# Eight weight halves of layer two's modulation: from the routing stage to the border of the layers

## The reference

```
silu_c, silu_cc = silu(c), silu(c_ctx)
for l in range(2):
    sh1, sc1, g1, sh2, sc2, g2 = split(silu_c @ w_mod[l] + b_mod[l], 6)     # the same for silu_cc
    u = h * (1 + sc1) + sh1                    # input of the token mixer
    h = layer_norm(alpha * h + g1 * token_mixer(u), ...)
    u2 = h * (1 + sc2) + sh2                   # input of the experts
    h = layer_norm(alpha * h + g2 * grouped_moe(u2), ...)
```

## Time and profile before

| | |
|---|---|
| median of 3 runs | 1628.79 us (1627.73 to 1631.53) |
| the profiled execution, its own time | 1631.92 us |
| its span (first to last instruction) | 1630.1 us |
| experts of layer one | 685 to 972 us |
| border: last product to layer two's first product | 972 to 996 us |
| mean granted clock of TensorE | 0.979 |

### The profile page before, as it was taken

How to read it: one execution, slowest core, us unless ns; L and a number is a source line. 1 busy time by engine, 2 the same in 40 slices (tenths; PEclk the granted TensorE clock), 3 DMA queues, 4 the chain that set the end, 5 groups by cost and what they waited for, 6 DMA issues and landing times.

```text
span 1630.1 us, 31680 instructions
## 1 busy us (share of the span) xinstructions
PE 1526.6 (94%) x13300; PEld 977.2 (60%) x13300; DVE 871.1 (53%) x1553; ACT 371.3 (23%) x893; POOL 272.4 (17%) x303
## 2 busy tenths in 40 slices
PE   6999999899999999898999886999999998999984
PEld 2454576564444468665666455767678887566642
DVE  3159946576777743652336437494552126554445
ACT  1100047541000010422222122003651002121211
POOL 0300000101112300043334330000000000543321
PEclk9999999999999999999999997999999998999998
DMA  9533220105857952999669968443125467999993
GB/s 338 176 103 94 78 68 27 49 30 180 277 151 249 319 209 80 354 414 391 235 270 400 414 273 304 143 120 99 47 59 190 144 220 284 375 415 414 414 415 137
DMA packets 147455, 365.23 MB, mean 224 GB/s; under 512 B 11265, under 2 KB 90729, under 8 KB 130419
## 3 DMA queue, kind: packets, MB, share of 16 engines
q1 hardware_dynamic: 125536, 296.86, 49.1%
q0 software_dynamic: 19328, 60.62, 11.0%
q10 hardware_dynamic: 2451, 5.73, 1.2%
HBM read 356.66 MB, written 10.62 MB: 225 GB/s over the span
## 4 chain that ended last, share of the span: by engine, by line
PE 66%; DVE 5%; DMA 5%; ACT 2%; SPq 1%; issue 1%; POOL 1%; DVEq 0%; ACTq 0%; POOLq 0%
PE psum L1166 64%; DMA yab<-in_moe_w_gu 3%; DMA arena<-in_moe_w_gu 1%; SPq L931 1%; PE psum L1703 1%; DVE ring L2772 1%; PE psum L1450 0%; DVE st L2197 0%; DMA yab<-ys 0%; DVE H L2794 0%; DVE st L2198 0%; POOL qkT_mqk L1076 0%; PE psum L1272 0%; DVE H L2210 0%; ACT uT L1870 0%
## 5 line engine op out<-in xcount | busy, mean ns | idle before, releaser
L1166 PE MATMUL psum<-uT,ring 128*128 128x512 f32 (+1 forms) x1440 | 496.1, 503 | 6.3 <-DMA ring<-in_w_in 4.8
L1166 PEld LDWEIGHTS psum<-uT,ring 128*128 128x128 f32 x1440 | 273.9, 192 | 216.4 <-issue 194.7
L1166 PE MATMUL psum<-ring,mo_tok 128*32 128x256 f32 x4992 | 312.9, 385 | 22.5 <-DVE ring L2772 22.2
L1166 PEld LDWEIGHTS psum<-ring,mo_tok 128*32 128x32 f32 x4992 | 158.8, 111 | 126.1 <-DVE ring L2772 30.1
L1166 PE MATMUL psum<-ring,v_tok 128*32 128x256 f32 x2496 | 150.1, 381 | 0.5 <-ACT v_tok L2119 0.5
L2350 DVE SCALAR_TENSOR_TENSOR convT<-upad_extra,cwT,convT 128x512 f32<-128x512 f32 (+1 forms) x240 | 132.4, 614 | 2.1
L1166 PEld LDWEIGHTS psum<-ring,v_tok 128*32 128x32 f32 x2496 | 82.3, 111 | 54.3 <-issue 1.7
L1166 PE MATMUL psum<-ring,uT 128*128 128x256 f32 (+1 forms) x576 | 113.1, 357 | 0.0
L1166 PEld LDWEIGHTS psum<-ring,uT 128*128 128x128 f32 x576 | 99.4, 191 | 15.4 <-issue 4.2
L1166 PE MATMUL psum<-yab,ring 128*128 128x512 f32 (+1 forms) x256 | 85.2, 486 | 0.0
L1166 PE MATMUL psum<-qkT_mqk 32*128 32x256 f32 (+5 forms) x752 | 81.3, 410 | 2.8 <-DVE qkT_mqk L2733 0.9
(11 more groups left out here) (364 smaller groups left out, 1635.2 us busy)
## 6 DMA issues: line engine op xcount, KB each, us to landing
ring<-in_w_in SPq DMA_DIRECT2D x104, 512.0 KB, 4.9
uT<-in_moe_w_gu SPq DMA_DIRECT2D x22, 1024.0 KB
yab<-in_moe_w_gu SPq DMA_DIRECT2D x21, 1024.0 KB, 19.5
arena<-in_moe_w_gu SPq DMA_DIRECT2D x21, 1024.0 KB, 20.3
ring<-in_w_mod SPq DMA_DIRECT2D x32, 512.0 KB, 9.8
mv_tok<-in_w_mod POOLq DMA_DIRECT2D x32, 512.0 KB, 5.3
convT<-in_w_mod POOLq DMA_DIRECT2D x32, 512.0 KB, 5.5
qkT_mqk<-in_moe_w_gu SPq DMA_DIRECT2D x14, 1024.0 KB, 19.0
```

What stands on the lines that cost most here:

```text
L1166: return nc.tensor.matmul(dst, lhsT, rhs, start=start, stop=stop)
```

## The change

The eight halves leave the routing. They are loaded after the last expert weights of layer one: seven into buffers which are spent by then (`BORDER`: `constants`, `values`, `tokens` = the gathered token rows `convT`, `rows`, `uT0`, `uT1`, `told`) and one through the ring. PE multiplies all eight after the last block and the gate rows. `keep_rows(4)` on ACT follows its gate rows; on DVE `modulation(4)` and the fold of w = 2 stand ahead of `add_experts`. The fold of w = 3 stays in the routing, so it now comes before that of w = 2 (`FOLDS`). With the halves gone, the first expert's pairs take their places in the ring, and the buffer `rows` moves from the end of the staging order to the fifth place, free once the scores are there. On POOL, the reload of `constants` for layer two waits for the columns of group 4.

```diff
-    ["constants", "yab0", "yab1", "values", "uT0", "uT1", "arena0", "arena1", "told", "rows"],
+    ["constants", "yab0", "yab1", "values", "rows", "uT0", "uT1", "arena0", "arena1", "told"],
...
+BORDER = dict(zip(MOD_HALVES[4], ["constants", "values", "tokens", "rows", "uT0", "uT1", "told"]))
+FOLDS = (1, 3, 5, 4)
...
-            for x in MOD_HALVES[4] if l == 0 else []:
-                used_modulation(x)
             for x in range(NS):
                 stream.append((("expert", l, x), w_used[x], blk_base[l] + n_blocks[l]))
+            for x in MOD_HALVES[4] if l == 0 else []:
+                if x not in BORDER:
+                    used_modulation(x)
...
                 elif name == "rows":
-                    wait_ready(sp, "modt", 4)
+                    wait_ready(sp, "scores", l)
+                    wait_ready(sp, "modt", 3)
...
+            def load_border_modulation():
+                for x, name in BORDER.items():
+                    m, u, half = x
+                    if name == "tokens":
+                        for i in range(2):
+                            sp.wait_ge(quads_ready[i], quad_base[0] + n_quads[0])
+                    else:
+                        last = max(n for n in range(N_STAGED) if stage_of(0, n) == name)
+                        sp.wait_ge(w_loaded[last % NP], 16 * (2 + last // NP))
+                    sp.dma_start(border[name].rearrange("p (k n) -> p k n", k=4),
+                                 wmod[m][:, 4 * half:4 * half + 4, u * 512:(u + 1) * 512]).then_inc(border_loaded[x], 16)
...
                     load_expert(l)
                     at += NS
+                    if l == 0:
+                        load_border_modulation()
...
                     pool.wait_ge(down_ready, blk_base[l] + nb)
+                    wait_ready(pool, "modt", 4)
                     for dst, src in reloaded:
...
# TensorE: modulation(x) waits for border_loaded[x]; its calls and modulation_columns(4) leave the routing
-                    modulation(MOD_HALVES[4][h])
...
-                    modulation(MOD_HALVES[4][2])
...
-                    for x in MOD_HALVES[4][3:]:
-                        modulation(x)
...
-                    pe.wait_ge(mod_kept, len(MOD_GROUPS))
+                    pe.wait_ge(mod_kept, len(MOD_GROUPS) - 1 + l)
...
-                    modulation_columns(4)
...
                     gate_rows(1, G2)
+                    for x in MOD_HALVES[4]:
+                        modulation(x)
+                    modulation_columns(4)
...
# ScalarE
-                    keep_rows(4)
...
                     gate_rows(1)
+                    keep_rows(4)
...
# VectorE
-                    modulation(4)
-                    for g in (3, 4):
-                        wait_drained(dve, "modt", g)
-                    for w in (2, 3):
-                        fold_norm(w)
+                    wait_drained(dve, "modt", 3)
+                    fold_norm(3)
...
                 if l < DEPTH - 1:
+                    modulation(4)
+                    wait_drained(dve, "modt", 4)
+                    fold_norm(2)
                     for h in range(nt // 2):
                         for t in (2 * h, 2 * h + 1):
                             add_experts(t)
```

More of the change, by code:

```diff
@@ L370, in psum_order @@
         order += [("table", l)]
+        order += [("g2", l, c) for c in range(nt) if l == 0]
         order += [("modt", 4)] if l == 0 else []
-        order += [("g2", l, c) for c in range(nt) if l == 0]
     place, uses, turn = {}, [0] * ROTATED, 0
@@ L587, in build @@
         staging["rows"] = upad_extra[:, N_PAD - D:N_PAD + D]
+        border = {**staging, "tokens": convT[:, :, :].rearrange("p a b -> p (a b)")}
         ln_rows = mo_tok[:, :, :, :].rearrange("p a b c -> p (a b c)")
@@ L675, in build @@
         w_staged = {name: sem(f"staged_in_{name}") for name in staging}
+        border_loaded = {x: sem(f"border_modulation_loaded_{name}") for x, name in BORDER.items()}
         constants_reloaded = sem("constants_reloaded")
@@ L1209, in modulation @@
                     s = MOD_GROUPS[g].index((m, u))
-                    wait_slot(pe, "mod", *x)
+                    if x in BORDER:
+                        pe.wait_ge(border_loaded[x], 16)
+                        w = border[BORDER[x]].rearrange("p (k n) -> p k n", k=4)
+                    else:
+                        wait_slot(pe, "mod", *x)
+                        w = slot_wide(slot_of("mod", *x))
                     if g and (s, half) == (0, 0):
@@ L1215, in modulation @@
                                   cT[:, 4 * half + q, MOD_AT - 2 * s:MOD_AT - 2 * s + 32],
-                                  slot_wide(slot_of("mod", *x))[:, q, :],
+                                  w[:, q, :],
                                   (s, half) == (0, 0), (s, half) == (len(MOD_GROUPS[g]) - 1, 1))
@@ L1613, in _ @@
                     done(last, *key)
-                    if l == 0:
-                        modulation(MOD_HALVES[4][h])
                 for x in range(nt // 2):
@@ L1625, in _ @@
                     natural(t)
-                if l == 0:
-                    modulation(MOD_HALVES[4][2])
-                else:
+                if l:
                     gate_rows(1, G2)
@@ L1684, in _ @@
                 done(last, "table", l)
-                if l == 0:
-                    modulation_columns(4)
-                final = uses_until(("modt", 4) if l == 0 else ("table", l))
+                final = uses_until(("table", l))
                 pe.wait_ge(drained[G_BANK[0]], final[G_BANK[0]])
@@ L1882, in norm_and_modulate @@
                         norm_std(w, 0)
-                    act.wait_ge(folded, w + 2 if w else 1)
+                    act.wait_ge(folded, FOLDS[w])
                     for h in range(tiles // 2):
@@ L2298, in modulate @@
                 def modulate(which):
-                    dve.wait_ge(folded, 2 * l + which + 2 if l or which else 1)
+                    dve.wait_ge(folded, FOLDS[2 * l + which])
                     tiles = nt if which else TT
```

## The result

The changed kernel takes 1642.78 us as the median of 5 runs (1639.29 to 1646.15), the kernel before 1627.73 us beside it (1625.84 to 1631.53). The ratio is 1.0091, with a 95% interval of 1.0076 to 1.0106: slower by some 15 us. A later pairing on one chip gave 1643.07 and 1.0109 (1.0088 to 1.013). The profiled execution took 1646.15 us, with a span of 1644.4.

The account below looks back on a forecast made before the run. Bound by the chain that ended last, PE carrying 66% of the span. Terms -1.1 + 2.7 - 6.8 + 19.4 = +14.2 us on the profiled 1631.9 give 1646.1, the median 3.1 lower: 1643.0, range 1632 to 1650.

Parts of the forecast that it names:

- Halves and columns out of the routing: Layer one's routing: removing the halves from PE's waits gains nothing, removing the columns before the first block gains 1.1 us.
- The clock in the gap: PE idle before `first_quad`: the clock falls to half and the slow start costs 2.7 us, bounds 0 and 3.2.
- Relief of the DMA: Before the experts: earlier expert loads remove the early stalls and the slow stretch behind them, gaining 6.8 us; later stalls stay.
- The gathers, with their long rows, gave up nearly nothing: Border: beside SP's loads the four gathers still land within 11.2 us, so the halves end when all is through.
- Rival A: Border: the queues share, halves end at 992 or a little before, the routing's clock doesn't fall; 1638 us; chance 0.16.
- The last half's landing: Border: the halves end once all bytes are through at 410 GB/s, taken as 994 us, bounds 992 to 997.
- The tail: Border, from the last half's landing to DVE's start: matmuls, copy, columns, bias and fold, 5.5 us with PE at half clock.
- the border's term: Border: DVE starts at 999.5 in place of 980.1, a loss of 19.4 us, bounds 5.4 and 22.
- B: Border: SP's loads served first, the gathers wait, landing before 981.5; 1625 us; chance 0.09 together with D.
- C: Before the experts: the DMA's lead is used up before 736, so early stalls stay; 1650 us; chance 0.08.
- D: Border: the change doesn't delay DVE, needing the last half by 976.6, 587 GB/s; chance 1%, counted with B.

Follow-up runs that it names:

- e3: Changed kernel with twenty small keep-busy matmuls on PE ahead of `first_quad` in layer one's routing, run on its own: 1646.12 us, ratio 1.0115.
- e9: Same edit as e3 (keep-busy matmuls ahead of layer one's `first_quad` in the changed kernel), run again beside e8: 1641.9 us, ratio 1.0094.
- e4: Kernel before, without the eight halves' loads and waits; their multiplications stay in the routing on the identity matrix: 1622.51 us, ratio 0.9971.
- e1: Changed kernel with DVE's modulation, wait and fold placed behind the sums and norms of the first pair of tiles: 1634.41 us, ratio 1.0037.
- e8: The changed kernel once more, with no edit: 1643.07 us.
- e11: Changed kernel in which SP issues its loads for layer two only when the eighth half has landed: 1642.72 us, ratio 1.0108.
- e12: Changed kernel with the edits of e1 and e11 together: 1632.82 us, ratio 1.0044.
- e2: Changed kernel loading only 32 of 512 columns of each half, all matmuls, copies and waits kept: 1670.11 us, a total that can't be compared.
- e10: Changed kernel in which SP issues the seventh and eighth half only when the four gathers have landed: 1648.9 us, ratio 1.014.
- e6: Changed kernel with only four halves at the border, four in the routing, and DVE's bias and fold behind the first tile's sums: 1624.56 us, ratio 0.9985.
- e5: Changed kernel with four halves kept in the routing with their columns and only four loaded at the border: 1626.48 us, ratio 0.9995.

## Why the prediction was right, and where two of its steps were not

**Halves and columns out of the routing: right.** No wait appeared where they had been, and `first_quad` is as far from the mark as before (24.98 and 25.05 us), so the halves had cost nothing there. The first block stands 11.55 us behind `first_quad`'s start, against 10.40 before: 1.8 from the clock, less 1.06 for the columns, and 0.4 in the table and the hand-over.

**The clock in the gap: right, over-sized.** I gave 2.7 us; `first_quad` lost 1.8 (9.16 for 7.38), and e3 and e9 gave 1.8 to 2.1 of it back. I had let the clock fall 2.4 us into the gap, as behind the gate rows, and had counted 5.4 us of busy time at half. In the kernel after it fell with the start of the gap: 0.89 over 668 to 669, 0.50 from 669 to 679, 0.99 over 679 to 681. So only 3.7 us of `first_quad` stood in it.

**Relief of the DMA: right.** The early waits and the slow stretch behind them went, the late ones stayed. In 684 to 760 DVE's copies waited 8.4 us for staged loads before and 0.2 after; pair 19's copy waited for none. The sum up to the gate rows was -1.1 + 2.7 - 6.8 = -5.2, the traces give -5.8, and e4, with no fall of the clock but with the columns, -6.5.

**"The gathers, with their long rows, gave up nearly nothing": wrong.** They landed after 7.8, 12.0 and 16.2 us. The DMA queues of the kernel after from 976 to 984 us (packets, MB, share of 16 engines; q10 is ACT's, q1 SP's):

```profile
q10 hardware_dynamic: 349, 2.58, 78.1%
q1 hardware_dynamic: 394, 0.77, 25.7%
```

The two queues moved nearly as many packets, 349 and 394, but of 7.4 KB and 2.0 KB. So the gathers kept three quarters of the bytes and gave up one quarter. Counted from 3 us behind the gathers' issue, the same 8 us of e1, e3, e8, e9, e11 and e12 have 350 to 361 packets against 361 to 393. This agrees with the Trainium skill (DMA: Bandwidth & Descriptors, "Queues, rings and completion order"), by which a DMA engine goes round between its queue rows packet by packet. I had read the landings of the earlier trace rows as though load on the other queue had been there from the start; SP's loads were issued only at 982.64, 7.5 us after the first gather (975.17), when 2.44 of the gathers' 4.19 MB had moved. It did no harm to the sum, since whoever goes first, the last half lands when all bytes are through. Rival A had the sharing right, but equal bytes wrong, and so no 2 us.

**The last half's landing: 3.5 us later than my account.** From the gate rows, 994 - 972.3 is 21.7 us; measured, 25.2 (992.04 - 966.86), and 25.0 in e8. In the prediction's times that is 997.5, just outside its bounds of 992 to 997. 0.7 us of the 3.5 I had taken off: the sum gave 994.7, and I took 994. For the rest, I had divided all bytes by one rate, 410 GB/s, and e11 shows what that leaves out. The 16 DMA engines finish unevenly: shares of 0.90, 0.64 and 0.15 in three windows of 2 us are some 2.5 us of idle time up to the landing. Layer two's loads going by add up to 0.9 us, of which not all is clear of the spread. **The tail** behind the landing was right: 5.2 us (992.04 to 997.22) for 5.5, with PE at half clock. So the border's term was 19.4 and measured 22.5, a term under-sized by 3.1.

**What came back, which no step had: -2.8 us.** Layer two's second transposes took 3.11 us before and 1.97 after; PE's clock from 1340 to 1400 us (a stretch of work that comes some 13 us later in the kernel after, so that each window holds its one fall) was 0.91 before:

```profile
1340.00:1400.00 60.00, 52.00 (x499) 41.12 (x498) 37.93 (x102) 14.46 (x28) 12.93 (x10) 0.91 0.70 266
```

and after:

```profile
1340.00:1400.00 60.00, 53.49 (x386) 46.12 (x388) 32.55 (x103) 13.66 (x22) 2.80 (x5) 0.97 0.68 256
```

I don't ascribe this to the change. The stretch between the start of those transposes and layer two's `first_quad` is 372.4 us before and 368.7 after, but 372.2 in e1 and 368.2 in e12, two kernels alike up to one wait. It isn't excluded either: e4, built on the kernel before, has 372.3, and all other traces of kernels built on the changed one have 368.2 to 369.9. So the total, 1643.0 for 1642.78, fits better than its terms, and that closeness is luck: the border was 3 us short, and 3 us came back elsewhere. The sign and the mechanism held, and the size of both large terms within 3 us.

**The rivals.** Of A, the queues did share, but the routing's clock fell. B (SP first) needed a landing before 981.5; in the prediction's times it was 997.5. C (no relief) is excluded by the waits. D needed DVE undelayed; e2 shows that even with a sixteenth of the bytes it would have been 5.5 us late.

## What to carry to other kernels

A load that is moved behind the last of a long series isn't free merely because the DMA falls idle there. Set its bytes, and those of every transfer that arrives meanwhile, against the time until the first consumer, and add the uneven finish of the DMA engines (some 2.5 us here). If they don't fit, move only the part that does (here half), and put the engine's wait for it as late in its program as the first real use.

Two terms that cancel look like accuracy, so compare each stage from a common mark before trusting a total.

## What the runs showed of the hardware that I had not expected

- Two queues with work for the same DMA engines shared packets, not bytes: 349 packets of 7.4 KB and 394 of 2.0 KB in 8 us, and much the same in six other traces. The throughput stayed at 416 GB/s from 980 to 984.
- Under that load a small scatter's landing slows as well. Timeline of POOL in the kernel after, its last scatter; ACT could issue the gathers only at 972.93, 5.3 us after this start, where before it took 2.1. It was 5.3 us in e1 and e8 and 6.8 in e10.

```profile
967.58 0.97 POOL L1127 DMA_INDIRECT ys<-qkT_mqk,y_row  x1 [1.69 <-ACT qkT_mqk L2161]
```

- The length of an idle gap alone doesn't tell whether the clock falls. In e3 PE idled 1.82 us before `first_quad` and kept 1.00 (7.41 us for it); in e6 it idled 1.76 us at the same place, and the clock fell:

```profile
674.43 8.92 PE L1193 MATMUL psum<-qkT_mqk,arena 128*128 128x128 f32 x64 [1.76 <-DVE qkT_mqk L2742]
```

```profile
669.00:679.00 10.00, 7.52 (x55) 6.43 (x44) 9.31 (x29) 2.08 (x3) 0.53 (x1) 0.83 0.97 341
```

What PE had done before the gap differed: twenty keep-busy matmuls in one; two halves, a group's columns and four keep-busy matmuls in the other. But the program alone doesn't decide it either. e5 has the same matmuls there as e6, and in its trace the clock fell on the halves' matmuls and was back in time:

```profile
665.62 3.46 PE L1193 MATMUL psum<-ring,cT 128*32 128x512 f32 x16
...
672.07 7.41 PE L1193 MATMUL psum<-qkT_mqk,arena 128*128 128x128 f32 x64 [0.24 <-DVE qkT_mqk L2742]
```

So one trace can't say what a gap of 2 us costs, and what decides where the fall lands was not tried.
